# Large-table expert layer: one 512-column moving operand for both halves of the activations, from pair 17 on

## The reference, cut to what matters

```python
q = (xt @ wq).reshape(T, PEER_HEADS, 2, PEER_DQ_HALF)
s1 = jnp.einsum('thd,nd->thn', q[:, :, 0], k1)
s2 = jnp.einsum('thd,nd->thn', q[:, :, 1], k2)
v1, i1 = lax.top_k(s1, PEER_TOPK)
v2, i2 = lax.top_k(s2, PEER_TOPK)
...
eidx = jnp.take_along_axis(cidx, pos, axis=-1).reshape(T, PEER_HK)
gate = jax.nn.softmax(sc.astype(jnp.float32), axis=-1).astype(x.dtype).reshape(T, PEER_HK)
...
    ub = jnp.take(u_tab, ib, axis=0)
    act = jax.nn.gelu(jnp.einsum('td,tkd->tk', xb, ub), approximate=False)
    vb = jnp.take(v_tab, ib, axis=0)
    return jnp.einsum('tk,tkd->td', gb * act, vb)
```

## Time and profile before

| | us |
|---|---|
| median of 3 runs (lowest to highest) | 3005.5 (3003.89 to 3008.38) |
| the profiled execution | 3004.97 |
| its span in the trace | 3003.2 |

### The profile page before, as it was taken

How to read it: one execution, slowest core, us unless ns; L and a number is a source line. 1 busy time by engine, 2 the same in 40 slices (tenths; PEclk the granted TensorE clock), 3 DMA queues, 4 the chain that set the end, 5 groups by cost and what they waited for, 6 DMA issues and landing times.

```text
span 3003.2 us, 47922 instructions
## 1 busy us (share of the span) xinstructions
PE 2935.1 (98%) x17398; PEld 2568.8 (86%) x17398; DVE 2193.7 (73%) x4100; ACT 1841.1 (61%) x2980; POOL 1110.4 (37%) x945
## 2 busy tenths in 40 slices
PE   8999999998999999999999999999999999999998
PEld 7778888776788887899999988887799999988887
DVE  4589999345899976497776577776579677577777
ACT  5668888444788865556666555554555666555554
POOL 4520000431100005688777510113678877711110
PEclk9999999999999999999999999999999999999999
DMA  7369999542899973467666777775447666777776
GB/s 232 117 237 369 371 371 372 191 147 88 296 366 375 368 257 123 142 190 221 203 203 202 234 243 245 241 241 181 145 146 227 210 204 201 210 250 242 239 241 206
DMA packets 203994, 701.72 MB, mean 234 GB/s; under 512 B 23602, under 2 KB 24754, under 8 KB 203504
## 3 DMA queue, kind: packets, MB, share of 16 engines
q1 hardware_dynamic: 170640, 619.07, 61.9%
q10 hardware_dynamic: 21056, 40.08, 3.6%
q0 software_dynamic: 12064, 39.52, 3.4%
HBM read 659.78 MB, written 38.80 MB: 233 GB/s over the span
## 4 chain that ended last, share of the span: by engine, by line
PE 92%; DVE 4%; ACT 1%; DMA 1%; issue 1%; POOL 0%; DVEq 0%; ACTq 0%; SPq 0%
PE ps L604 91%; PE ps L620 1%; DVE hrow L105 1%; DVE arena L95 1%; DVE ps L105 1%; DVE arena L105 1%; DMA rawb<-in_s_T 0%; DVE hL L95 0%; POOL splitb L545 0%; DMA hrow<-in_x_rows 0%; ACT hH L159 0%; ACT arena L159 0%; ACT arena L161 0%; ACT splitb L518 0%; DMA rawb<-in_ab_out 0%
## 5 line engine op out<-in xcount | busy, mean ns | idle before, releaser
L518 ACT ACTIVATE splitb<-rawb 128x512 fp32r<-128x512 f32 (+1 forms) x1306 | 826.8, 639 | 738.0 <-PE ps L604 627.4
L545 POOL TENSOR_TENSOR splitb<-rawb,splitb 128x512 fp32r<-128x512 f32 x739 | 952.7, 1302 | 738.8 <-ACT splitb L518 727.5
L604 PE MATMUL ps<-hH,splitb 128*128 128x256 f32 x5248 | 986.5, 284 | 8.7 <-DVE hL L95 2.7
L604 PEld LDWEIGHTS ps<-hH,splitb 128*128 128x128 f32 x5248 | 836.0, 192 | 15.9 <-issue 10.1
L604 PE MATMUL ps<-splitb,hid 128*128 128x512 f32 x3444 | 788.6, 389 | 0.0
L604 PEld LDWEIGHTS ps<-splitb,hid 128*128 128x128 f32 x3444 | 646.4, 188 | 134.9
L604 PE MATMUL ps<-hL,splitb 128*128 128x256 f32 x2624 | 744.2, 284 | 0.0
L545 DVE TENSOR_TENSOR splitb<-rawb,splitb 128x512 fp32r<-128x512 f32 (+1 forms) x567 | 393.8, 714 | 179.5 <-ACT splitb L518 178.5
L604 PEld LDWEIGHTS ps<-hL,splitb 128*128 128x128 f32 x2624 | 505.1, 192 | 0.4
L604 PE MATMUL ps<-experts_r 128*128 128x512 f32 (+3 forms) x1390 | 332.0, 386 | 7.4 <-ACT experts_r L159 6.6
L604 PEld LDWEIGHTS ps<-experts_r 128*128 128x128 f32 (+1 forms) x1390 | 251.8, 188 | 62.4 <-issue 7.0
(11 more groups left out here) (171 smaller groups left out, 3205.6 us busy)
## 6 DMA issues: line engine op xcount, KB each, us to landing
rawb<-in_peer_u SPq DMA_DIRECT2D x256, 512.0 KB, 4.0
rawb<-in_peer_v SPq DMA_DIRECT2D x256, 512.0 KB, 4.2
experts<-in_moe_gu SPq DMA_DIRECT2D x228, 512.0 KB, 5.4
experts<-in_moe_d SPq DMA_DIRECT2D x108, 512.0 KB, 5.4
rawb<-in_moe_gu SPq DMA_DIRECT2D x92, 512.0 KB, 5.4
aux<-spill POOLq DMA_DIRECT2D x128, 256.0 KB, 4.4
spill<-gb ACTq DMA_DIRECT2D x120, 256.0 KB, 4.1
rawb<-in_moe_d SPq DMA_DIRECT2D x52, 512.0 KB, 5.4
```

Of the source, the lines that this page charges most:

```text
L518: self.eng.activation(S.split(m)[0], S.raw(n)[:, off:off + w], ACT.Copy).then_inc(S.hi.sem, S.hi.step(("half", m)))
L545: self.eng.tensor_tensor(l, raw, h.bitcast(F32), ALU.subtract).then_inc(self.low.sem, self.low.step(("half", m), *([("raw", n)] if last el ...
L604: return self.eng.matmul(o, w, x, start=start, stop=stop)
```

## The change

From pair 17 on (`WIDE`) a tile has a bank of its own. `hH` and `hL` of a block now lie side by side in one tensor `hx`, and `proj_wide` multiplies the high weights with both in one matmul of 512 moving columns: columns 0 to 255 of the bank collect high by high and low by high, columns 256 to 511 high by low. The two parts have to be added afterwards. `act_part` (ScalarE) copies columns 256 to 511 to the buffer, `dve_early` (VectorE) adds columns 0 to 255 to them in place, and `act_spill` (ScalarE) takes the Gelu of the pair from the buffer to the buffer and sends it off.

In the names below, i is a pair and j (0 or 1) a tile of it. ScalarE now runs: two splits, `act_part(i-1, 1)`, the gate copies of tile (i, 0), Gelu and transfer of pair i-1, two splits, `act_part(i, 0)`, the gate copies of tile (i, 1). VectorE runs after the gate work of tile (i, 0) the addition for tile (i-1, 1), and after that of tile (i, 1) the addition for tile (i, 0): always that of the tile before.

```diff
+WIDE = 17
...
-        hH = sb("hH", 2048, F32R)
-        hL = sb("hL", 2048, F32R)
+        hx = sb("hx", 4096, F32R)
...
-        self.hH = hH[:, :].rearrange("p (k t) -> p k t", k=8)
-        self.hL = hL[:, :].rearrange("p (k t) -> p k t", k=8)
+        self.hx = hx[:, :].rearrange("p (k a t) -> p k a t", k=8, a=2)
+        self.hH, self.hL = self.hx[:, :, 0, :], self.hx[:, :, 1, :]
...
+    def proj_wide(self, o, *names):
+        S = self.S
+        for i in range(2):
+            m = self.half
+            self.wait_ge(S.hi, "half", m)
+            h, l = S.split(m)
...
+            self.low(m)
+            for k in range(4):
+                both = S.hx[:, 4 * i + k, :, :].rearrange("p a t -> p (a t)")
+                if (i, k) == (1, 3):
+                    self.mm(o[:, 0:256], wl[:, k, :], S.hH[:, 4 * i + k, :], False, False)
+                    ins = self.mm(o, wh[:, k, :], both, False, True)
+                else:
+                    self.mm(o, wh[:, k, :], both, i + k == 0, False)
+                    ins = self.mm(o[:, 0:256], wl[:, k, :], S.hH[:, 4 * i + k, :], False, False)
+            self.out(ins, ("half", m), *(names if i else ()))
+            self.half += 1
+        self.tile += 1
...
         for p in range(64):
-            b = pe.open("p.u", n, p)
+            b = None if p >= WIDE else pe.open("p.u", n, p)
             for j in range(2):
-                pe.proj(b[:, 256 * j:256 * j + 256], ("p.u", n, p))
+                if p >= WIDE:
+                    pe.proj_wide(pe.open("p.u", n, p, j), ("p.u", n, p, j))
+                else:
+                    pe.proj(b[:, 256 * j:256 * j + 256], ("p.u", n, p))
...
     def act_early(self, act, i):
...
+        if i > WIDE:
+            self.act_part(act, i - 1, 1)
         for k in twos(2 * i):
             self.act_high_sum(act, k)
+        if i > WIDE:
+            self.act_spill(act, i - 1)
         act.fed()
...
+        if i < WIDE:
+            self.act_spill(act, i)
+        else:
+            self.act_part(act, i, 0)
+        for k in twos(2 * i + 1):
+            self.act_high_sum(act, k)
+        if i == 63:
+            self.act_part(act, i, 1)
+            self.act_spill(act, i)
...
+    def act_spill(self, act, i):
...
+        else:
+            act.wait_ge(S.vdone, "p.us", n, i, 1)
+            act.act(r, r, ACT.Gelu, ("p.ue", n, i))
         act.wait_ge(S.acted)
         act.eng.dma_start(S.spill.ap()[n, i, :, :], r).then_inc(ring.sem, ring.step(("spill", i)))
...
+    def act_part(self, act, i, j):
+        S, n = self.S, self.layer
+        act.wait_ge(S.product, "p.u", n, i, j)
+        if j == 0:
+            act.wait_ge(S.load(f"spill{n}_{i % 2}"), "spill", i - 2)
+        act.cp(self.early(i)[:, 256 * j:256 * j + 256], S.bank["p.u", n, i, j][:, 256:512], ("p.ul", n, i, j))
+
+    def dve_early(self, dve, i, j):
+        S, n = self.S, self.layer
+        r = self.early(i)[:, 256 * j:256 * j + 256]
+        dve.wait_ge(S.acted, "p.ul", n, i, j)
+        dve.tt(r, S.bank["p.u", n, i, j][:, 0:256], r, ALU.add, ("p.us", n, i, j), ("drained", ("p.u", n, i, j)),
+               own=False)
...
                     if k >= 2:
                         self.dve_sum(dve, k - 2)
+                if 2 * p + j > 2 * WIDE:
+                    self.dve_early(dve, p + j - 1, 1 - j)
```

## The result

The changed kernel is slower, and by more than forecast: median 3096.51 us of 6 runs (3088.32 to 3101.65) against 3006.36 us of 6 runs of the kernel before. The ratio is 1.0295, interval 1.0276 to 1.0314. The forecast was 3060, range 3030 to 3085: right in direction and in its main mechanism, wrong in size. The profiled execution took 3088.51 us with a span of 3086.6, 83.4 above the span before. The six runs fall in two groups, 3088 to 3093 us at a mean granted clock of 0.994 and 0.995, and 3100 to 3102 at 0.988 to 0.990; the profile is one of the lower group.

The account below looks back on a forecast made before the run. TensorE was taken to bound the kernel. Per layer 38.2 us lost in stalls less 10.5 gained on matmuls makes 27.7 slower, both layers 55; 3005 + 55 = 3060 us, range 3030 to 3085.

Parts of the forecast that it names:

- What TensorE gains: TensorE's product blocks: one start in three saved, 0.346 us a block instead of 0.360, 21 us over 1504 blocks.
- The chain behind D: From a tile's products done (D), through split, copy, addition and selection matrices: next products at D + 4.58, not 3.49.
- 35 couples stall: Gate matrix: a two-step tile behind a one-step tile is 1.09 us late, 35 times, 38.2 us lost a layer.
- The third tiles with two steps: A two-step tile behind such a couple: permitted at 7.83, TensorE arrives at 7.83, no wait.
- The gate stretches together: Each layer's stretch building the gate matrix: 38.2 us of stalls less the block gain, 29.1 us slower.
- The step that failed: Last six pairs of a layer, without gate work: no such wait of TensorE; costed at a 1.3 us gain.
- ScalarE on time, banks, GpSimd: Added work hidden: ScalarE on time by 0.1 us, four banks suffice, GpSimd's 5.2 us a pair below 5.54.
- The clock between the stalls: TensorE's granted clock while the gate matrix is built: the prediction is wrong if it falls between the waits.
- Rival 3: Stalls in all 70 couples bring TensorE's clock down: 42 to 119 us more, 3140 taken; chance 0.05.

Follow-up runs that it names:

- e3: e2 with each block again as three matmuls of 256 columns, undoing the wide operand alone; 3013.94 us, ratio 1.0021 to the kernel before.
- e6: The changed kernel with every ScalarE copy of a second sum done twice; 3141.56 us, ratio 1.0436 to the kernel before.
- e2: The changed kernel with ScalarE's copy of a tile's second sum one tile sooner; 3002.65 us, ratio 0.9981 to the kernel before.
- e8: e1 with ScalarE's Gelu and transfer of a pair also one tile later, behind the gate copies; 3019.36 us, ratio 1.0038 to the kernel before.
- e11: The changed kernel, late copy kept, but wide for pairs 17 to 57 only; 3071.75 us, ratio 1.0208 to the kernel before.
- e4: The changed kernel with the copy sooner from pair 58 on only; 3078.78 us, ratio 1.0242 to the kernel before.
- e7: The changed kernel with VectorE, in the last six pairs, making low weight halves and first low gated half ahead of additions; 3085.14 us, ratio 1.0266.
- e1: The changed kernel with VectorE's addition one tile later while the gate matrix is built; 3054.91 us, ratio 1.0162 to the kernel before.
- e5: e2 with VectorE, in the last six pairs, making low weight halves and first low gated half ahead of additions; 3007.97 us, ratio 0.9998.
- e9: e2 but with the wide operand for pairs 17 to 57 only; 2989.31 us, ratio 0.9941 to the kernel before.

## Why the prediction was wrong, step by step

- *What TensorE gains*: right in kind, too large. 0.350 us a block (e3) for 0.346; 14 us in place of 21. Neither width in a stretch of its own gave the cost of the two in turn. The Trainium skill ("TensorE: Matmul & The Clock Gate", Back-to-back issue gap) gives N/2.4 + 2.5 ns as the gap of isolated matmuls, by which a start would be worth an estimated 2.5 ns; the 9.6 ns of e3 lie between that and the 14 of the forecast.
- *The chain behind D*: right, all eight steps (trace), and that it is the loop is shown by lengthening it (e6) and by opening it in two places (e2, e8).
- *35 couples stall*: right. From tile 34 on the counts of steps are 1, 2, 1, 2, 1, 2, 1, 2, 2, 1, 2 (the list ahead of the prediction lacks a 1, 2), which makes the 36 couples of the forecast. TensorE goes through the first of them, tiles 34 and 35, without a wait, and waits at the second step in each of the other 35. The third tiles with two steps, ten in a layer, do not wait, as the forecast had it with nothing to spare. One wait was not foreseen, so that each layer has 36 in all. The copy for tile 34 came behind a split that waited for its weights, and TensorE waited for the single step of tile 36, which was to be free; the second step of tile 37 then waited only 0.15 us. ScalarE, then TensorE:

```profile
1413.87 0.63 ACT L518 ACTIVATE splitb<-rawb 128x512 fp32r<-128x512 f32 x1 [2.47 <-DMA rawb<-in_peer_u]
...
1411.87 0.40 PE L604 MATMUL ps<-aux_r 128*128 128x256 f32 x2
1412.10 0.40 PE L604 MATMUL ps<-hid 128*128 128x256 f32 x2
...
1416.40 0.51 PE L604 MATMUL ps<-aux_r 128*128 128x256 f32 x2 [1.12 <-DVE aux_r L105]
```

- *The gate stretches together*: 38.2 - 81 x 8 x 0.014 = 29.1 us each were forecast, 31.8 and 31.2 came. With e3's 9.6 ns in place of the 14 the same sum gives 38.2 - 6.2 = 32.0: the loss in the couples was right, and the gain was mis-sized. That is 4.8 of the 28 us that the profiled execution lies above the forecast.
- *The step that failed*: "the last six pairs of a layer, without gate work, have no such wait". They were costed at a gain of 1.3 us a layer and lost 9.9 and 9.2: 21.8 of the 28. The chain was worked out for the selection matrices and not asked of the other things that VectorE makes for TensorE behind an addition: the low weight halves from pair 60 on and the first low half of the gated values. In the first layer the three waits are 1.52 + 2.76 + 3.64 = 7.9 us, and the low clock between the last two costs some 1.5 more. e11 shows that this part is separate, e4 that the late copy is behind 7.4 and 6.1 us of it, e7 that VectorE's order causes the first two of its three waits. A remainder of 1.7 and 2.3 us stays in e2 even with the sooner copy: there TensorE's only wait is the 2.28 us in front of the first second product (first layer), and VectorE's low half for it (1705.93) stands right behind the very last addition (1705.47), which had waited 2.15 us for its copy, as e2's expectation had it.
- *ScalarE on time, banks, GpSimd*: right; with e2 all of their work is still there and the time is not.
- *The clock between the stalls*: right for the couples, it stays at 1.00 from 1430 to 1660 us, with waits of 0.8 to 0.9 us mostly 7.4 us apart. Rival 3 was not asked of the last six pairs, and there it came true in part: the clock fell behind the wait of 2.76 us (shown above), and again during that of 3.64:

```profile
1748.00:1750.00 2.00, 0.01 (x1) 0.04 (x1) 1.65 (x4) 1.30 (x4) 0.00 (x0) 0.61 0.02 6
1750.00:1752.00 2.00, 2.00 (x5) 1.61 (x6) 2.00 (x4) 1.49 (x2) 0.55 (x1) 0.50 0.55 160
```

- The median lies another 8 us above the profiled execution. No profile caught one of the changed kernel's longer executions. But e6's profiled execution has the same mean clock as they have, 0.988, and it lost much ahead of anything that the change touches: its first gate matmul starts at 1418.77 us, for 1408.82 in the changed kernel's profile. From 660 to 800 us, the changed kernel and then e6:

```profile
660.00:800.00 140.00, 123.12 (x671) 100.13 (x670) 97.96 (x209) 78.72 (x134) 24.78 (x16) 0.99 0.41 149
660.00:800.00 140.00, 125.52 (x653) 102.48 (x652) 89.52 (x202) 72.71 (x130) 26.23 (x17) 0.91 0.37 129
```

  That the changed kernel's own longer executions lose their time there is likely and not shown.

## What to carry to other kernels

A new instruction on an in-order engine can cost the lateness of what stands behind it, and not only its own 0.42 us. So list everything that this engine still makes for the bound engine, in every stretch that the change reaches, and work out for each how late the new wait lets it be. When such a wait binds, move the thing waited for sooner, as e2 does with one tile; moving the waiting instruction later made something else wait for it (ScalarE's Gelu in e1, the first gated values in e5 and e7), and it took a second move, in e8, to open that. And keep a change to the stretch where it pays: e9 gave up the wide operand in the last 12 tiles of each layer and was the fastest of all.

## What the runs showed of the hardware

512 and 256 columns in turn take 0.350 us from start to start of a pair of matmuls (e3 against e2), though the rows of either width alone suggest 0.346. In e2's trace the median distance from a 512-column start to the 256-column one behind it is 0.233 us, and 0.117 us from there to the next.

36 waits of TensorE in a layer, most of 0.8 to 0.9 us and 7.4 us apart, left the granted clock at 1.00, where I had given its fall a chance of 0.05. Longer waits were not all alike. Those of 1.52 us in the changed kernel and of 2.57 us in e8 (in front of 1685.00 us) left the clock at 1.00; those of 2.15 and 2.76 us in the changed kernel were followed by 0.50, the level of 1.2 GHz; and during that of 3.64 us it fell before TensorE started again. So these runs show that waits of this size can cost the clock, and give no length that decides it.
